# One core, one decoder stack: the pooling stage in two halves of the tokens, and VectorE's order in the two mixing stages

## The reference

```python
# first block, layer 1: h is the layer-normed sum of the experts' output and the residual of layer 0
def pool_mixer(x, w_in, w_grp, ls, w_out):
    u = (x @ w_in).reshape(B, S, N_POOL_GROUPS, POOL_GROUP_DIM)       # 4 groups of 256 channels
    for g, w in enumerate(POOL_WINDOWS):                              # 2, 4, 8, 16
        cs = jnp.cumsum(ug, axis=1)                                   # sums over the last w tokens
        mean = (cs - lag) / jnp.minimum(count, float(w))[None, :, None]
        feats.append(mean - ug)
    y = jnp.einsum('bsgc,gcd->bsgd', p, w_grp).reshape(B, S, D_MODEL) * ls
    return y @ w_out

# second block, for each of its two layers
shift, scale, gate = jnp.split(silu(c) @ ada_w[l] + ada_b[l], 3, axis=-1)
mixed = jnp.concatenate([r_o * silu(rz), m_o * silu(mz), g_o * silu(gz)], axis=-1)
x = x + gate[:, None, :] * (mixed @ w_out[l])     # r_o retention, m_o attention, g_o gated linear attention
# behind the last layer: rms_norm(x, final_norm)
```

## Time and profile before

| what | value |
|---|---|
| median of 3 runs | 3649.71 us (3647.54 to 3656.63) |
| the profiled execution | 3647.19 us, span 3645.3 us |
| busy share of the span, PE / PEld / DVE / ACT / POOL | 95% / 74% / 66% / 52% / 12% |
| pool stage, first to last matmul | 1293.35 to 1524 us |
| first mixing stage | 2789 to 2981 us |
| last mixing stage | 3448 to 3645 us |

### The profile page before, as it was taken

How to read it: one execution, slowest core, us unless ns; L and a number is a source line. 1 busy time by engine, 2 the same in 40 slices (tenths; PEclk the granted TensorE clock), 3 DMA queues, 4 the chain that set the end, 5 groups by cost and what they waited for, 6 DMA issues and landing times. The chain is left out here.

```text
span 3645.3 us, 53840 instructions
## 1 busy us (share of the span) xinstructions
PE 3449.7 (95%) x18229; PEld 2681.6 (74%) x18229; DVE 2415.8 (66%) x3956; ACT 1881.2 (52%) x3175; POOL 453.2 (12%) x499
## 2 busy tenths in 40 slices
PE   8998889899999979998999999899998999999988
PEld 7885658688888835586888887487886767787766
DVE  3226877699988855647998887763176755407675
ACT  3215662288888720114888886232267733216674
POOL 0000002021111130000211111400001310000032
PEclk9999999899999999998999999999999999999999
DMA  6532224399999976444999998643232343424241
GB/s 247 218 146 94 81 90 170 112 392 381 376 374 378 348 263 233 166 177 166 384 379 378 378 370 302 239 173 122 98 91 84 110 144 124 157 70 129 70 127 64
DMA packets 413217, 766.16 MB, mean 210 GB/s; under 512 B 107609, under 2 KB 162545, under 8 KB 411000
## 3 DMA queue, kind: packets, MB, share of 16 engines
q1 hardware_dynamic: 390008, 711.93, 54.6%
q0 software_dynamic: 22752, 50.93, 3.8%
q10 hardware_dynamic: 288, 1.05, 0.1%
HBM read 643.00 MB, written 152.72 MB: 218 GB/s over the span
## 5 line engine op out<-in xcount | busy, mean ns | idle before, releaser
L253 DVE TENSOR_TENSOR experts_gate_lo<-weights_gate,experts_gate_hi 128x1024 fp32r<-128x1024 f32 x256 | 302.9, 1221 | 84.2 <-ACT experts_gate_hi L249 83.5
L249 ACT CAST experts_gate_hi<-weights_gate 128x1024 fp32r<-128x1024 f32 x256 | 257.4, 1056 | 131.8 <-DMA weights_gate<-in_moe_w_gate_dram 97.5
L253 DVE TENSOR_TENSOR experts_down_lo<-weights_down,experts_down_hi 128x1024 fp32r<-128x1024 f32 x256 | 296.1, 1219 | 27.2 <-ACT experts_down_hi L249 27.2
L253 DVE TENSOR_TENSOR experts_up_lo<-weights_up,experts_up_hi 128x1024 fp32r<-128x1024 f32 x256 | 295.9, 1218 | 0.3
L318 PE MATMUL project_acc<-project_wh,project_hh 128*128 128x512 f32 (+2 forms) x768 | 285.9, 372 | 0.0
L320 PE MATMUL project_acc<-project_wh,project_hl 128*128 128x512 f32 (+2 forms) x768 | 281.9, 367 | 0.0
L319 PE MATMUL project_acc<-project_wl,project_hh 128*128 128x512 f32 (+2 forms) x768 | 281.8, 367 | 0.0
L249 ACT CAST experts_up_hi<-weights_up 128x1024 fp32r<-128x1024 f32 x256 | 257.4, 1057 | 13.6 <-DMA weights_up<-in_moe_w_up_dram 11.6
L249 ACT CAST experts_down_hi<-weights_down 128x1024 fp32r<-128x1024 f32 x256 | 254.7, 1053 | 8.8 <-DMA weights_down<-in_moe_w_down_dram 8.6
L2780 ACT COPY project_row<-project_acc 128x512 f32<-128x512 f32 (+2 forms) x96 | 51.8, 540 | 363.6 <-PE project_acc L320 363.6
L318 PE MATMUL experts_gp<-experts_gate_hi,experts_xh 128*128 128x512 f32 x512 | 201.7, 394 | 12.5 <-DVE experts_xl L253 12.2
(11 more groups left out here) (551 smaller groups left out, 8308.7 us busy)
## 6 DMA issues: line engine op xcount, KB each, us to landing
weights_gate<-in_moe_w_gate_dram SPq DMA_DIRECT2D x256, 512.0 KB, 12.0
weights_up<-in_moe_w_up_dram SPq DMA_DIRECT2D x256, 512.0 KB, 13.4
weights_down<-in_moe_w_down_dram SPq DMA_DIRECT2D x256, 512.0 KB, 11.5
scratch_y<-qkv_zero SPq DMA_DIRECT2D x48, 512.0 KB, 4.5
pool_shared<-in_ada_w_dram SPq DMA_DIRECT2D x16, 1536.0 KB, 6.7
scratch_proj<-project_row SPq DMA_DIRECT2D x64, 256.0 KB, 2.0
head_store<-in_attn_w_qkv_dram SPq DMA_DIRECT2D x48, 256.0 KB, 3.7
scratch_qkv<-qkv_row SPq DMA_DIRECT2D x48, 256.0 KB, 2.1
```

The source lines that it names most:

```text
L249: return act.copy(hi, src)
L253: return dve.tensor_tensor(lo, src, hi.bitcast(F32), ALU.subtract)
```

## The change

**Pool stage in halves.** Step n = 0 to 7 is the first 512 tokens, n = 8 to 15 the second (`tile_at`), channel tiles in falling order, so the groups go from the window of 16 down to that of 2; `group_at` numbers eight half groups G. `channels(n)` needs only the tiles of its half. `pool_u`, `pool_pT` and `pool_y` have two buffers of half the length; the last 16 columns of the first half are kept in `tails` and copied in front of the second. `pool_w` is loaded by group, four loads of 1 MB in rows of 256 columns, and the first channel product waits for one of them. The loads of `pool_wg`, the scale and the counts go out behind the store of tile 3. Combine uses two of the four `pool_rp` banks from tile 4 on, since `outputs` takes the other two. Adds of the modulation begin behind window 3.

```diff
+    def bank_of(self, n):
+        late = n // 2 >= self.NARROW
+        return 2 + n % 2 if late else n % len(self.banks)
...
-        u = ph.sb("u", [P, PADW + SEQ])
-        s = ph.sb("s", [P, 2, PADW + SEQ])
+        u = ph.sb("u", [P, 2, PADW + HALF])
+        s = ph.sb("s", [P, 2, PADW + HALF])
+        tails = ph.sb("tails", [P, KC, PADW])
...
-        ADDS = (3, 2, 3, 2, 3, 2, 1, 0)
+        ADDS = (0, 0, 0, 1, 1, 2, 1, 2, 1, 2, 1, 2, 1, 2, 0, 0)
+        W_LOADS = (0, 2, 4, 5)
...
-                for i in range(TILES - 1):
-                    if i + 2 < TILES:
-                        cb.sums(nc, pe, i + 2)
+                for i in range(HT):
+                    cb.sums(nc, pe, i + 2)
                     transposes(i)
-                channels(0, 0)
-                transposes(TILES - 1)
-                channels(0, 1)
...
+                for n in range(2):
+                    channels(n)
+                    cb.sums(nc, pe, n + 2 + HT)
+                    transposes(n + HT)
+                for G in range(GROUPS_):
+                    if G + 1 < GROUPS_:
+                        channels(CG * (G + 1))
+                    if G == GROUPS_ - 1:
+                        m.total(nc, pe, 1, mod_bank)
+                    outputs(G)
+                    if G < 1:
+                        transposes(TILES - 2)
+                    if G == 4:
+                        m.total(nc, pe, 0, mod_bank)
+                    if G == 5:
+                        m.turn_back(nc, pe, K, 0, mod_bank)
+                    if G == GROUPS_ - 1:
+                        m.turn_back(nc, pe, K, 1, mod_bank)
+                    if G + 1 < GROUPS_:
+                        channels(CG * (G + 1) + 1)
+                    if G < 1:
+                        transposes(TILES - 1)
...
                 cb.add(dve, cch, 0)
-                for i in range(1, TILES + 1):
+                for i in range(1, HT + 2):
+                    cb.add(dve, cch, i)
+                    norm(i - 1)
                 dve.wait_ge(small_in, 16 * (2 * NG + 1))
+                for n in range(2):
+                    window(n)
+                    cb.add(dve, cch, n + HT + 2)
+                    norm(n + HT + 1)
+                for G in range(GROUPS_):
+                    outputs(G)
+                    for n in range(CG * (G + 1), min(CG * (G + 2), STEPS)):
+                        window(n)
+                        if n == CG:
+                            norm(TILES - 1)
+                        adds(n)
```

**Mixing stages.** Two steps of VectorE move ahead of the first residual:

```diff
                     if has(i):
                         mean_squares(i)
                         gated(i)
+                    if has(i + 1):
+                        gla_operands(i + 1)
+                    if final and has(i - 2):
+                        final_mean(i - 2)
                     if i == 1:
                         dve.wait_ge(gate_loaded, 32 if final else 16)
                     if has(i - 1):
                         residual(i - 1, 0)
-                    if has(i + 1):
-                        gla_operands(i + 1)
-                    if final and has(i - 2):
-                        final_mean(i - 2)
```

More of the change, by code:

```diff
@@ L2277, in _ @@
                         cb.load(sp, i + cb.HB)
-                    load_w(i)
+                    if i in W_LOADS:
+                        load_w(NG - 1 - W_LOADS.index(i))
                     cb.store(sp, i)
[L2280 to L2284, removed]
@@ L2288, in _ @@
                 at = 0
-                for ct in range(KC):
-                    for n in range(at, at + ADDS[ct]):
+                for k in range(STEPS):
+                    for n in range(at, at + ADDS[k]):
+                        if n == 0:
+                            sp.wait_ge(cb.rp_ready, 2 * TILES)
                         m.load(sp, n)
[L2292 to L2296, removed]
@@ L2439, in adds, with norm @@
-                def adds(ct):
-                    for n in range(sum(ADDS[:ct]), sum(ADDS[:ct + 1])):
-                        m.add(dve, n)
-                dve.wait_ge(small_in, 16 * (2 * NG + 1))
-                for ct in range(CG):
-                    window(ct)
-                    adds(ct)
-                for g in range(NG):
-                    outputs(g)
-                    if g + 1 < NG:
-                        for ct in range(CG * (g + 1), CG * (g + 2)):
-                            window(ct)
-                            adds(ct)
+                def norm(i):
+                    cb.norm(dve, cch, i, (tp_ready, 2 * (i - 2) + 2))
@@ new lines, in outputs @@
+                def outputs(G):
+                    g = group_at(G)[1]
+                    if G > 1:
+                        dve.wait_ge(stored[G % 2], 16 * (G // 2))
+                    for t in range(0, HT, 2):
+                        dve.wait_ge(y_ready, HT // 2 * G + t // 2 + 1)
+                        dve.tensor_tensor(ysb[:, G % 2, t:t + 2, :], yp[:, t // 2, :].rearrange("p (a c) -> p a c", a=2),
+                                          lsb[:, g * PG:(g + 1) * PG].unsqueeze(1).to_broadcast([P, 2, PG]), ALU.mult).then_inc(y_done, 1)
@@ new lines, in adds @@
+                def adds(k):
+                    for n in range(sum(ADDS[:k]), sum(ADDS[:k + 1])):
+                        m.add(dve, n)
+                cb.add(dve, cch, 0)
+                for i in range(1, HT + 2):
+                    cb.add(dve, cch, i)
+                    norm(i - 1)
+                dve.wait_ge(small_in, 16 * (2 * NG + 1))
+                for n in range(2):
+                    window(n)
+                    cb.add(dve, cch, n + HT + 2)
+                    norm(n + HT + 1)
```

214 lines of the change are left out of this document (116 added, 98 removed).

## The result

The changed kernel takes 3615.89 us (median of 4 executions, 3612.51 to 3619.15) against 3649.43 before: a ratio of 0.9904 with a 95% interval of 0.9887 to 0.9922, about 35 us less where 28.4 was forecast. With all the executions of the later experiments the means are 3648.8 (46 of before) and 3615.0 (12 of the changed kernel): 33.8 us, with a standard error of 0.8.

A forecast was written before the change was run, and what follows sets the result against it. TensorE, busy 95% of the span, was taken as the bound. Gains of 15.0 (pool stage), 4.6 (first mixing stage) and 8.8 (last) sum to 28.4: 3649.7 - 28.4 = 3621 us, range 3615 to 3632.

The forecast's parts named there:

- five waits and 0.92: Last mixing stage: five TensorE waits for the copy of kw go, 7.9 us, plus 0.92 from the first tile: 8.8 us.
- the pool stage's 15.0: Pool stage in halves: last transpose at 1505.5 instead of 1520.53, 15.0 us less, if TensorE waits for nobody in between.
- what follows stays as it is: End of pool stage: the copy, three small stores and last mix-row store behind the last transpose stay unchanged.
- The wait for the bank: Pool stage: with two banks, one sum waits for the previous tile's add; priced at nothing, below 2 us if norm early.
- The tight place: Pool stage, second modulation sum behind total(0): TensorE has 16.7 us of work, VectorE 17.2; wait taken as 0, at most 0.5.
- rival 1: Pool stage: late ada_w loads or VectorE, at 10 us a landing; 6 us lost, 3627; chance 0.13.
- rival 4: Pool stage: same loads at 15.5 us, 32.5 lost, 3654, slower than before; decides from 14.9 us a landing; chance 0.02.
- the sign of being wrong: Pool stage: VectorE waits for DMA pool_shared above 3 us more than twice would show the forecast wrong.
- The low clock behind the totals: Pool stage: outputs behind the two column totals stay slowed by the lower clock, 2.9 and 1.9 us more.
- 0.92 us a tile: First mixing stage: operands moved into the residual's wait save TensorE 0.92 us in five tiles, 4.6 us.
- Rival 3: First mixing stage: TensorE comes 0.92 earlier and waits for state s_g instead; 4.6 us lost, 3626; chance 0.08.
- Rival 2: Last mixing stage: GpSimd blocks VectorE for both products in normalization and scaling; 4.5 us lost, 3626; chance 0.11.

The follow-up runs named there:

- the one-stage kernel: The changed kernel with VectorE's new order in the last mixing stage alone, the first keeping the old order; 3617.96 us, a mean 3.1 more than the changed kernel.

## Why the prediction was right and wrong, point by point

Over all profiles, in us:

| stretch | old, mean (range, profiles) | new, mean (range, profiles) | less | forecast |
|---|---|---|---|---|
| pool stage up to the next stage's first product | 234.6 (232.8 to 236.1, 5) | 216.6 (214.2 to 219.7, 6) | 18.0 | 15.0 |
| first mixing stage and the projections behind it | 492.7 (491.9 to 493.4, 5) | 487.9 (486.3 to 488.7, 9) | 4.8 | 4.6 |
| last mixing stage | 185.8 (182.3 to 188.7, 4) | 174.7 (172.8 to 175.6, 9) | 11.1 | 8.8 |

The six new ones of the first line leave out the kernels with later weights and wide totals. Of its 18.0, some 0.4 come back as a wait for `out_x` in the next stage, and about 0.6 in the rest of that stage and the routing behind it, so that 17.0 are left. The sum is 32.9, against 33.8 by the executions' means.

- **The step that failed** is the size of two terms, and with it the way the sum was made: each was read from one profiled execution and taken from the median of all. The larger miss is the last mixing stage's 8.8 us, "five waits and 0.92". It measured 11.1 by the profiles and 12.7 (standard error 1.8) by the executions. The 8.8 is the gain over an execution whose last stage ran with the clock up (183.5 and 182.3 against 174.7 are 8.8 and 7.6). In two of four profiles with the old order the loop also loses some 5 us to the clock, in none of nine with the new one. The prediction looked for what the waits last and never for what they do to the clock behind them, though it had priced just that behind the totals. The other is the pool stage's 15.0, of which 17.0 came, for the reasons in the next point. Together they are 4.3 of the 5.4 us by which the gain exceeds the forecast.
- **How far the clock is shown.** The two profiles with the loss are both of kernels with the changed pool stage, and the two without it are both of before, so the profiles alone leave open that the new pool stage brings it on. Against that: the eleven executions with before's pool stage and the new operands' place gained 16.4 us (standard error 0.9), 3.0 more than the 13.4 forecast for both mixing stages, and the kernel with longer waits, which has before's pool stage, lost clock in the same loop. Over the 46 executions of before, time and mean granted clock go together (correlation -0.73, 1.9 us for 0.001), so much of their scatter is clock, though not only that of this loop.
- **Pool stage.** The mechanism held: the first channel product 44.8 us after the stage's start (mean of six) where 1337.9 meant 44.6, the work behind it 166.7 where 167.6 was summed. The surplus of 3.0 in the table is in small pieces. The work was summed 0.9 too long. Before's own figures were a little short of its mean (the product at 64.3, mean of five 64.9; the work 162.9, mean 163.2). And "what follows stays as it is" was wrong by 1.4: from the last transpose to the next stage's first product it takes 5.05 us in all six, 6.45 in all five of before, of which 0.4 is lost again in the wait for `out_x`. The last store of mix rows is half as large now, which would explain it; this wasn't tried.
- **The wait for the bank** was priced at nothing. It came, 4.32 us (1323.92), because DVE waited 6.4 us for the residual rows of tile 3. It cost nothing all the same, for the reason given: the norm that tile 3's transposes need stands behind the same add and was as late.
- **The tight place** behind total(0) is where the forecast put it: 0.69 us of wait for outputs(5), a little over the bound of 0.5, and 0.33 for outputs(6). Rivals 1 and 4 (late loads) didn't come: the landings were 7.7 us in the median, under the 10 on which rival 1 is worked out, and 13.4 at most, under the 14.9 from which rival 4 decides. DVE did wait for these loads eight times, 13.5 us in all, and twice above 3 us (3.43 and 3.31), just short of the sign of being wrong; PE's only waits for the windows are the two named.
- **The low clock behind the totals** stayed, as the sum had it: 1.5 and 2.8 us behind them where 2.9 and 1.9 were taken over from before, and the totals themselves 7.32 and 7.66.
- **First mixing stage.** 0.92 us a tile came exactly, 4.8 in all; by the executions of the one-stage kernel 3.1, which with a standard error of 0.9 doesn't contradict it. Rival 3 fell: the wait for the state stayed at 0.20 a tile.
- **Rival 2 fell.** The scaling starts at 3535.67 and takes 2.32 us: 1.24 for which GpSimd's first product still runs (to 3536.91) and 1.08 of its own. The second product, which starts 0.04 us before that point, doesn't hold it up: it takes 1.59 us itself, where the shortest of the eight in that stage takes 0.61, and ends 0.47 behind the scaling. The Trainium skill (SBUF — State Buffer, section "SBUF: two separate sides") says that one engine fully blocks the other for a whole instruction; the trace agrees, with the scaling held up by the first product and the second product by the scaling; it is one product that DVE loses in the new order too, not both.

On the clock, the rows show it falling with PE busy the whole time, in one-column totals (1494 to 1502, 0.50, under a total from 1491.24 on), and in a loop whose waits are 1.67 us. The Trainium skill (TensorE: Matmul & The Clock Gate, "A second HAM failure mode: psum-queue depth-cycling") tells of a kernel whose many short waits between groups of products make the clock fall and rise again; the last stage in the old order agrees in two of four profiles. The same page ("What's actually happening") says that the chip's look at the activity runs free of the kernel, so that one kernel differs from run to run; two of four profiles is compatible with that, and too few to show it.

What stays open: less time at the lower level in every second execution should raise the mean granted clock by some 0.0007. With before's pool stage it doesn't: 0.9785 for before (46 executions) as well as for the eleven with only the mixing stages changed, each with a standard error of 0.0002. With the pool stage changed it goes from 0.9797 (old order in the last stage, ten executions) to 0.9809 (twelve), each with an error of 0.0004. So the mean clock fits the clock's part with the changed pool stage and not with before's, where only the times show that the mixing term was too small. And no run shows why the wait costs the clock in one execution and not in the next.

## What to carry to other kernels

Read the stage that a term rests on in more than one execution, or in the other kernels' profiles that share it, before the term is taken from the median of many: here the last mixing stage's term was 2 to 4 us short, in a loop where the clock is down at times, and the pool stage's 2. A short wait that repeats in every tile can be worth more than its sum. Operations moved into a wait that is there anyway took no time of their own here. Look at what the engine's busy time consists of as well: products of one column keep it busy and let its clock fall.

## What the runs showed of the hardware

- 24 products of one column (128x128 weights, fp32; two records each) take 5.4 to 8.2 us, and a stretch at the lower clock begins in them or within 0.2 us behind them in each of the twelve profiles that have them. Of 96 columns they take 5.50 and no such stretch comes, in two profiles. Up to there the columns are free.
- A wait of 1.67 us in each tile of 20.7 us was followed by lower clock in two of four profiles (10 us at 1.2 GHz, 5 us lost), one of up to 3.2 us by three stretches in one profile (17 us); with only waits of 0.2 us a tile there was no such stretch in nine.
- A VectorE operation of 1024 columns that meets two GpSimd products in a row takes 2.32 us instead of 1.28, and the second of the products 1.59 instead of 0.61: the times are those of two engines of which each waits for the one that came first.
- Before against itself, 11 against 15 executions: 1.0, 0.9991 to 1.0009. Single executions of it lie 17.5 us apart (3639.97 to 3657.50), those of the changed kernel 6.9 (3612.25 to 3619.15).

The lowest time is that of the kernel with wide totals, 3612.6 by the mean of five, 2.4 us below the changed one (standard error 1.1): little more than chance gives, though its profile says where the time went.
